# Splitting each chunk of weights with one VectorE operation of 2048 columns in place of two of 1024

## What is computed

```python
def first_block(...):                       # kinds: 0 retention, 1 conv, 2 gated linear attention
    for i in range(DEPTH):                  # DEPTH = 4
        u = rmsnorm(h, norm_gains[i, 0])
        y = retention(...) | conformer_conv(...) | gla(...)
        h = h + rmsnorm(y, norm_gains[i, 1])
        u = rmsnorm(h, norm_gains[i, 2])
        h = h + rmsnorm(sq_relu_mlp(u, mlp_w_up[i], mlp_w_down[i]), norm_gains[i, 3])
def sq_relu_mlp(u, w_up, w_down):
    return jnp.square(jax.nn.relu(u @ w_up)) @ w_down
```

## Time and profile before

| what | value |
|---|---|
| median of 3 runs | 2140.88 us |
| lowest, highest | 2139.97, 2141.39 us |
| the profiled execution | 2141.29 us |
| its span, first to last instruction | 2139.5 us |
| mean granted clock of TensorE | 0.999 |
| busy: PE, PEld, DVE, ACT, POOL | 99%, 84%, 67%, 55%, 6% |
| moved from HBM | 368.65 MB, 173 GB/s over the span |

### The profile page before, as it was taken

The page is one execution under the profiler, slowest core; times in us unless marked ns, Lnnn a source line. Parts: engine busy times, 40 slices in busy tenths (PEclk is TensorE's granted clock), DMA queues, the critical chain, the costliest instruction groups (busy, mean ns, idle before and its releaser), DMA issues.

```text
span 2139.5 us, 28814 instructions
## 1 busy us (share of the span) xinstructions
PE 2119.2 (99%) x11347; PEld 1790.0 (84%) x11347; DVE 1433.1 (67%) x2080; ACT 1170.1 (55%) x1727; POOL 122.8 (6%) x161
## 2 busy tenths in 40 slices
PE   9999999999999999999999999999999999999999
PEld 9888888868888878889888888877888888888887
DVE  7755765667666677657755755686755699675665
ACT  5565644636445645455565644666544566575443
POOL 0000200002000021000000200003000100000000
PEclk9999999999999999999999999999999999999999
DMA  8545755536555436665545666542755566513652
GB/s 279 189 148 166 238 185 189 189 96 209 191 185 180 158 99 219 197 196 181 167 146 182 177 195 197 177 158 68 218 187 195 182 176 180 179 59 119 212 185 95
DMA packets 190341, 371.57 MB, mean 174 GB/s; under 512 B 7184, under 2 KB 126432, under 8 KB 190080
## 3 DMA queue, kind: packets, MB, share of 16 engines
q1 hardware_dynamic: 185776, 358.70, 51.3%
q0 software_dynamic: 4432, 11.02, 2.5%
HBM read 368.65 MB, written 1.05 MB: 173 GB/s over the span
## 4 chain that ended last, share of the span: by engine, by line
PE 94%; DVE 4%; ACT 1%; issue 1%; POOL 0%; DMA 0%; DVEq 0%; ACTq 0%; POOLq 0%
PE PS L678 48%; PE PS L803 14%; PE PS L805 7%; PE PS L791 4%; PE PS L841 3%; PE PS L848 1%; DVE wlo L2124 1%; PE PS L740 1%; PE PS L742 1%; PE PS L1169 1%; PE PS L741 1%; PE PS L889 1%; PE PS L966 1%; PE PS L772 1%; PE PS L1448 1%
## 5 line engine op out<-in xcount | busy, mean ns | idle before, releaser
L2124 DVE TENSOR_TENSOR wlo<-raw,whi 128x1024 fp32r<-128x1024 f32 x658 | 786.4, 1225 | 165.3 <-ACT whi L1540 164.4
L1540 ACT ACTIVATE whi<-raw 128x1024 fp32r<-128x1024 f32 x680 | 697.4, 1053 | 311.8 <-PE PS L678 270.9
L678 PE MATMUL PS<-whi,U 128*128 128x512 f32 x1696 | 472.4, 394 | 4.8 <-DVE AR L2365 1.3
L678 PEld LDWEIGHTS PS<-whi,U 128*128 128x128 f32 x1696 | 316.1, 188 | 73.7 <-issue 9.0
L803 PE MATMUL PS<-U,whi 128*128 128x512 f32 x1344 | 334.4, 391 | 0.0
L803 PEld LDWEIGHTS PS<-U,whi 128*128 128x128 f32 x1344 | 246.9, 188 | 47.2
L2251 DVE TENSOR_TENSOR AR<-PS,AR 128x512 f32<-128x512 f32 x96 | 66.2, 690 | 293.9 <-ACT AR L1633 293.9
L678 PE MATMUL PS<-wlo,U 128*128 128x512 f32 x848 | 262.5, 391 | 0.0
L1633 ACT ACTIVATE AR<-PS 128x512 f32<-128x512 f32 x96 | 57.0, 594 | 348.8 <-PE PS L805 348.8
L678 PE MATMUL PS<-whi,fH 128*128 128x512 f32 x768 | 238.4, 392 | 0.9 <-DVE fL L2398 0.9
L678 PE MATMUL PS<-wlo,fH 128*128 128x512 f32 x768 | 237.2, 390 | 0.0
(11 more groups left out here) (351 smaller groups left out, 2234.3 us busy)
## 6 DMA issues: line engine op xcount, KB each, us to landing
raw<-in_mlp_w_up SPq DMA_DIRECT2D x64, 1024.0 KB, 5.5
raw<-in_mlp_w_down SPq DMA_DIRECT2D x64, 1024.0 KB, 4.9
raw<-in_ret_w_in SPq DMA_DIRECT2D x48, 1024.0 KB, 5.2
raw<-in_m_w_up SPq DMA_DIRECT2D x32, 1024.0 KB, 5.4
raw<-in_m_w_down SPq DMA_DIRECT2D x32, 1024.0 KB, 4.9
raw<-in_kv_w SPq DMA_DIRECT2D x24, 1024.0 KB, 5.3
raw<-in_ret_w_out SPq DMA_DIRECT2D x16, 1024.0 KB, 4.9
raw<-in_gla_w_in SPq DMA_DIRECT2D x12, 1024.0 KB, 5.2
```

The lines of the kernel that those rows point to most:

```text
L678: mm = e.matmul(bank(b + nb), a, w[:, nb * 512:(nb + 1) * 512], start=(begins and n < 2), stop=(ends and n >= 4))
L1540: e.activation(split_half(whi, i, x), raw_halves(i)[x], ACT.Copy).then_inc(HI.tick((i, x)), 1)
L2124: e.tensor_tensor(split_half(wlo, i, x), raw_halves(i)[x], split_half(whi, i, x).bitcast(F32), ALU.subtract).then_inc(LO.tick((i, x)), 1)
```

## The change

VectorE's two operations on the two halves of a chunk become one on the whole chunk. It waits for the second high half and then adds 2 to the counter at its end, so both halves' low parts are given free at the same moment. ScalarE's halves, GpSimd's chunks, and TensorE's waits are not changed. Since a chunk can no longer be split by halves, two places where a single half was put between other operations change: in DIFF, the half behind `combined(7)` goes with the other half of its chunk into the next `lo_of`, and in DIL the halves of one chunk that stood at steps 13 and 14 are both at step 14.

```diff
--- before.py
+++ after.py
@@ -2115,19 +2115,26 @@
         def dve_program(e):
             done = [0]
 
-            def lo_half():
-
-                i, x = divmod(done[0], 2)
+            def whole(w, i):
+                o = w[:, i % NS, :]
+                return o if plan[i][1] != "b" else o.rearrange("p (s t n) -> p s t n", s=2, t=8)
+
+            def lo_next():
+
+                i = done[0]
                 done[0] += 1
-                if (i, x) not in LO_SEAM.value:
-                    e.wait_ge(*HI[i, x])
-                    e.tensor_tensor(split_half(wlo, i, x), raw_halves(i)[x], split_half(whi, i, x).bitcast(F32),
-                                    ALU.subtract).then_inc(LO.tick((i, x)), 1)
+                if (i, 0) not in LO_SEAM.value:
+                    a = raw[:, i % NR, :]
+                    if plan[i][1] == "b":
+                        a = a.rearrange("p (t s n) -> p s t n", t=8, s=2)
+                    e.wait_ge(*HI[i, 1])
+                    LO.tick((i, 0))
+                    e.tensor_tensor(whole(wlo, i), a, whole(whi, i).bitcast(F32), ALU.subtract).then_inc(LO.tick((i, 1)), 2)
 
             def lo_to(n):
 
-                while done[0] < 2 * min(n, NCH):
-                    lo_half()
+                while done[0] < min(n, NCH):
+                    lo_next()
 
             def lo_of(i0, n):
                 lo_to(i0 + n - 1 + NS)
@@ -2960,8 +2966,8 @@
                         scaled(i + 3)
                     if i >= 2 and i % 2 == 0:
                         output(i // 2 - 1)
-                    if i in (13, 14):
-                        lo_half()
+                    if i == 14:
+                        lo_next()
                 output(7)
                 lo_to(first[S + 1])
                 seam(S)
```

## The result

The changed kernel takes 2161.91 us (median of 4 runs, 2160.60 to 2162.01) against 2140.6 us (4 runs) of the kernel before: 1.0097 times as long, 95% interval 1.0085 to 1.0109. That is 21.3 us slower; the forecast was 2158, with a range of 2150 to 2168. The profiled execution took 2162.01 us.

A forecast was written before the change was run, and what follows sets the result against it. TensorE, busy 2119.2 of 2139.5 us, was taken to bound the kernel. Delays of 5.9 + 0.6 + 3.45 + 6.0 + 0.6 + 0.5 + 0.2 = 17.3 us gave 2158 us against the median, range 2150 to 2168.

The forecast's parts named there:

- rival of VectorE's throughput: Rival: TensorE waits for VectorE's throughput, so the change is faster; 8 us won, 2133 us; chance 0.03.
- DIFF's heads: Term: in DIFF the pair at 1409.39 starts 0.81 us later, ahead of TensorE's wait on line 2762; 0.6 us.
- rival in which only direct waits count: Rival: what stands behind VectorE has unseen slack, leaving seams and start; 9.4 us, 2150 us; chance 0.10.
- RET's six steps: Term: three places each in RET0 and RET1 where TensorE waits for operations behind the split on VectorE; 6.0 us together.
- the whole is early enough everywhere: Rival: TensorE's queue hides the late first half; within 0.2% (4.3 us), at most 2145 us; chance 0.05.
- my sum: The prediction's main case, all terms added: 17.3 us, 2158 us, own range 2154 to 2162; chance 0.70.
- The start: Term: the kernel's first chunks, where whole low parts come later and the shift grows over chunks 0 to 2; 3.45 us.
- rival of the clock: Rival: clock falls in longer gaps at three seams and the start, 1.6 us each, 6.4 us more, 2165; chance 0.12.
- seams: Term: CONV, DIFF and DIL, with a second mixer chunk right behind; first half late, 1.95 us each, 5.9 us together.
- steady work: Claim: chunks are split 5 us and more before TensorE asks, hiding the delay; new waits mid-stage put at nothing.
- my own signs: Signs of being wrong: whole operation under 2.2 or above 2.36 us, clock under 0.99, new waits in a stage's steady middle.
- DIFF's terms: Terms in DIFF: its seam 1.95 us, the next chunk 0.6 us, and the heads 0.6 us.

The follow-up runs named there:

- late_shared: Changed kernel with two operations of 1024 columns again, both waiting for the second high half and released together behind the second: 2162.79 us, 1.0101 of the kernel before.
- best_whole: The orders of best_halves, with whole operations on 317 of VectorE's 329 chunks: 2136.74 us, 0.9980 of the kernel before.
- best_halves: halves_reordered, with the split also moved behind the last rotation of DIFF's keys and the low part of DIL's kv input: 2136.80 us, 0.9978 of the kernel before.
- late_own: As late_shared, both halves behind the second high half, but each with its own release: 2154.58 us, 1.0064 of the kernel before.
- whole_places_only: Whole operations only on the 20 chunks where the changed kernel's trace shows TensorE falling back, halves on the other 309: 2163.13 us, 1.0102 of the kernel before.
- whole_but_places: Changed kernel with halves on the 20 chunks where its trace shows TensorE falling back, whole operations on the other 309: 2143.21 us, 1.0010 of the kernel before.
- whole_reordered: Changed kernel with the split moved behind product_v(0), turn(0, 1) and turn(3, 1) in both retentions: 2151.69 us, 1.0049 of the kernel before.
- start_only: Whole operations on the first three chunks alone, halves everywhere else: 2145.12 us, 1.0019 of the kernel before.
- start_busy: As start_only, but TensorE multiplies ones by ones 20 more times ahead of its first product: 2145.60 us, 1.0022 of the kernel before.
- halves_reordered: The kernel before, halves everywhere, with the order of whole_reordered in both retentions: 2138.48 us, 0.9983 of the kernel before.
- moved_halves: The kernel before, halves everywhere, with only the change's two moves of place in DIFF and DIL: 2141.63 us, 1.0002 of the kernel before.

## Why the prediction was right, and what it missed

**The bound and the saving.** Right. TensorE bounds the kernel, the whole operation takes 2294 ns, and its saving (18.3 us of VectorE, 23 forecast) is absorbed in VectorE's waiting. The Trainium skill's remark (Perfetto Trace Analysis, Optimizing Scalar/DVE Operations) that smaller instructions may finish the work sooner, where an engine that isn't saturated causes bubbles on others, agrees with this case: VectorE at 67%, and the halves 21.3 us faster than the whole. What counts is the earlier start and release that halves allow, since late_shared has halves and loses as much. The idea that larger operations help is the rival of VectorE's throughput, and best_whole against best_halves settles it: 0 us. My fall of VectorE's busy time was 5 us too large. The group itself lost 786.4 - 754.0 = 32 us, and no other operation of VectorE gained: together they differ by 0.8 us. The rest is overlap. In the trace the record of an operation often begins before that of the one ahead of it ends, 103 us in all before and 71 now, and what overlaps counts once: the total of the durations fell by 50.6 us, the busy time by 32.3 us less.

**Where the delay lands.** Right in place and size: every row of the table that has a forecast is met to within 0.25 us. late_own and late_shared show that it is the wait for the second high half and the common release, not the operation; whole_places_only and whole_but_places that it is these chunks, but for one that hides behind the start and for 0.5 us in DIFF's heads. The rival in which only direct waits count falls: RET's six steps alone are 6.4 us, and whole_reordered takes them away. So does the one in which the whole is early enough everywhere.

**What was mis-sized.** The forecast was 3.7 us too low: inside its range, at the very end of the 2154 to 2162 that my sum had for itself. The misses nearly all go one way, so no luck of errors that cancel made the number. *The start*, 3.45 forecast and 5.03 in the profile. The difference is one stretch at the lower clock behind the gap of 2.6 us, with 1.5 us against the 1.6 that the rival of the clock gave for one. start_only has 3.55 without it. So the sum's term was right, and the rival was partly true, at one of its four spots: at the seams the gaps of 1.7 us left the clock at 1.00 in every profile. What the prediction says of this rival's row, the lower level half the time, is wrong: with the two levels 0.5 and 1.0, a mean of 0.53 over 3.40 us is the lower level nearly all the time. The cost it took was about right all the same. The Trainium skill (TensorE: Matmul & The Clock Gate, HAM oscillation) has idle gaps bring the engine back to the lower clock. Four of the six gaps of 2.2 us and more agree with that, the other two don't. Its example is a loop with longer waits than those of the seams in every turn, so the 2165 us that I put beside it were my reading, not the page's.

*GLA*, absent from the sum, 0.89 measured. I counted it as steady work, where "a chunk is split 5 us and more before TensorE asks for it". That is true of the chunk, but lines 2577 to 2585 stand behind two splits there, and TensorE's next product waits for the result of line 2585 (2592 now). By my own signs this was one of being wrong: a new wait inside a stage, where I had put nothing. The delay I should have carried through both splits is 1.01 - 2 x 0.07 = 0.87 us; timelines of the kernel before and of the changed one:

```profile
683.98 4.63 DVE L2124 TENSOR_TENSOR wlo<-raw,whi 128x1024 fp32r<-128x1024 f32 x4
688.53 0.69 DVE L2577 COPY AR<-PS 128x512 f32<-128x512 f32 x1
```

```profile
695.29 4.49 DVE L2132 TENSOR_TENSOR wlo<-raw,whi 128x2048 fp32r<-128x2048 f32 x2 [1.01 <-ACT whi L1540]
699.70 0.68 DVE L2584 COPY AR<-PS 128x512 f32<-128x512 f32 x1
...
701.98 0.47 PE L791 MATMUL PS<-U,whi 128*128 128x256 f32 x2 [0.68 <-DVE AR L2592]
```

*Handoffs*, the time from a result to the matmul that waited for it: seams 2.03 to 2.05 in place of 1.95, RET 1.07 in place of 1.0 a place, 0.7 us together. That the handoff is what they lack is my reading; no run takes it apart. With the clock and GLA that is 3.1 of the 3.4 us between 17.3 and 20.7; DIFF's terms hold the rest. TensorE's busy time, which I expected unchanged, rose by 4.0 us, 1.5 of them at the lower clock; the first matmuls behind a wait are shown longer (0.73 us for two, 0.62 elsewhere).

**What stays open.** Whether filling the gap at the start would keep the clock: start_busy overshot. And what decides whether the clock falls behind such a gap: six profiles show both outcomes. The remaining waits of TensorE on VectorE (lines 1305, 1296, 2518) weren't tried.

## What to carry to other kernels

Merging two operations saves one fixed cost, here 0.07 us, and delays the first result by the time of the second input and the second half, here 2.0 us. On an engine that waits for its inputs the first was worth nothing here, and the second costs what it exceeds the slack by, wherever a consumer with less slack is behind, directly or through the engine's order. Look at the boundaries between stages and at short operations queued behind the merged one. There the order was worth more than the size: moving the split behind what TensorE waits for gave 4.1 us between the medians, with halves or whole operations alike, as long as the places whose first half is wanted at once keep their halves.

## What the runs showed of the hardware

Behind gaps of TensorE of 2.2 (twice), 2.6 and 3.6 us the granted clock fell (0.50 for 3.4 us in the changed kernel), behind two of 3.17 us it didn't (1.00). Gaps of 1.65 to 1.94 us at the seams, in RET and in DIL left it at 1.00 in every profile. Yet in CONV, among several small gaps and one of 1.24 us, it fell in five of the fourteen profiles: the kernel before, the changed one, whole_places_only, halves_reordered and moved_halves, there for twice as long. The other nine have the same instructions there and no such stretch. So the length of the last gap alone doesn't decide it. A stretch is worth 1.3 to 1.5 us, so two executions of one kernel may differ by that much through it.
